# A mixture of experts streamed from memory: pairs of experts with 64 slots become quads with 32, and routing joins the experts' block

## The reference, cut to what matters

```python
N_EXPERT_GROUPS, EXPERTS_PER_GROUP, N_EXPERTS, TOP_K, D_EXPERT = 4, 8, 32, 2, 512
grp_prob = softmax(hf @ w_group_router + b_group_router);  grp_p, grp_idx = top_k(grp_prob, 1)
sel_logits = expert logits of the chosen group (8 of them)
top_p, top_i = top_k(softmax(sel_logits), 2)
gates = grp_p * top_p / sum(top_p)
# each expert over the tokens that chose it:
hid = silu(xb @ w_expert_gate[e]) * (xb @ w_expert_up[e])   # 1024 -> 512
y   = hid @ w_expert_down[e]                                # 512 -> 1024, times the gate, summed per token
x   = x + y
```

## Time and profile before

| | us |
|---|---|
| runs | 1523.35, 1523.48, 1530.56; median 1523.48 |
| span of the profiled execution | 1521.0 |
| its own end of `mix_part`, first ring load issued | 368.0 |
| routing block | 368.0 to 388.7 |
| expert block, to the next block's first work | 389.3 to 860.9 |
| TensorE busy in the whole span | 1428.1 (94%) |

### The profile page before, as it was taken

How to read it: one execution, slowest core, us unless ns; L and a number is a source line. 1 busy time by engine, 2 the same in 40 slices (tenths; PEclk the granted TensorE clock), 3 DMA queues, 4 the chain that set the end, 5 groups by cost and what they waited for, 6 DMA issues and landing times. The chain is left out here.

```text
span 1521.0 us, 23457 instructions
## 1 busy us (share of the span) xinstructions
PE 1428.1 (94%) x9837; PEld 1077.8 (71%) x9837; DVE 779.3 (51%) x1207; ACT 525.1 (35%) x726; POOL 2.9 (0%) x12
## 2 busy tenths in 40 slices
PE   6988996997799999999999799999999999999998
PEld 5988694997444444444444489789999898799997
DVE  4474765552311211211221259877777479777776
ACT  4542524332010010010000234754454455654443
POOL 0000000000000000000000000000000000000000
PEclk8999997997899999999999999999999999999999
DMA  7841000772999999999999554655664352655650
GB/s 247 267 141 38 20 4 25 221 234 118 388 421 421 421 420 421 421 421 421 421 421 420 200 175 144 167 148 172 192 193 146 119 194 84 194 168 178 193 168 28
DMA packets 192509, 349.75 MB, mean 230 GB/s; under 512 B 9164, under 2 KB 158833, under 8 KB 167570
## 3 DMA queue, kind: packets, MB, share of 16 engines
q1 hardware_dynamic: 191914, 347.59, 63.4%
q10 hardware_dynamic: 488, 0.62, 0.1%
HBM read 347.13 MB, written 3.43 MB: 230 GB/s over the span
## 5 line engine op out<-in xcount | busy, mean ns | idle before, releaser
L2616 DVE TENSOR_TENSOR w_lo<-expert_early,w_hi 128x2048 fp32r<-128x2048 f32 x72 | 164.8, 2291 | 29.3 <-ACT w_hi L2449 28.3
L1811 DVE TENSOR_TENSOR hT<-ps,hT 128x512 f32<-128x512 f32 x16 | 17.1, 1067 | 304.1 <-PE ps L1741 304.1
L1741 PE MATMUL ps<-expert_ring,w_slot 128*64 128x512 f32 x768 | 167.5, 592 | 0.0
L2449 ACT ACTIVATE w_hi<-expert_early 128x2048 fp32r<-128x2048 f32 x72 | 137.7, 1913 | 58.3 <-PE ps L2354 38.9
L1741 PEld LDWEIGHTS ps<-expert_ring,w_slot 128*64 128x64 f32 x768 | 55.6, 137 | 109.2 <-issue 109.2
L2316 PE MATMUL ps<-x_hi,w_hi 128*128 128x256 f32 x864 | 123.4, 286 | 4.6 <-DVEq L2759 4.6
L2316 PE MATMUL ps<-x_lo,w_hi 128*128 128x256 f32 x864 | 123.1, 285 | 0.3 <-DVE x_lo L2755 0.2
L2316 PE MATMUL ps<-x_hi,w_lo 128*128 128x256 f32 x864 | 121.4, 283 | 0.0
L2316 PEld LDWEIGHTS ps<-x_hi,w_hi 128*128 128x128 f32 x864 | 112.9, 192 | 8.8 <-DVEq L2759 5.0
L2316 PEld LDWEIGHTS ps<-x_lo,w_hi 128*128 128x128 f32 x864 | 112.5, 193 | 0.9 <-DVE x_lo L2755 0.8
L2316 PEld LDWEIGHTS ps<-x_hi,w_lo 128*128 128x128 f32 x864 | 111.7, 192 | 0.0
(11 more groups left out here) (487 smaller groups left out, 2263.0 us busy)
## 6 DMA issues: line engine op xcount, KB each, us to landing
expert_ring<-in_w_expert_up SPq DMA_DIRECT2D x48, 1024.0 KB, 17.6
expert_ring<-in_w_expert_down SPq DMA_DIRECT2D x48, 1024.0 KB, 20.4
expert_ring<-in_w_expert_gate SPq DMA_DIRECT2D x48, 1024.0 KB, 16.8
expert_early<-in_ffn_up SPq DMA_DIRECT2D x36, 1024.0 KB, 6.1
w_slot<-in_w_in SPq DMA_DIRECT2D x28, 1024.0 KB, 6.1
expert_early<-in_w_in SPq DMA_DIRECT2D x20, 1024.0 KB, 5.2
expert_early<-in_ffn_down SPq DMA_DIRECT2D x18, 1024.0 KB, 4.9
expert_early<-in_w_expert_gate SPq DMA_DIRECT2D x16, 1024.0 KB, 13.1
```

Source lines behind the costliest of these rows:

```text
L1741: mm = pe.matmul(m.ps[e * SLOTS:(e + 1) * SLOTS, b, :], x_pair[:, k, e * SLOTS:(e + 1) * SLOTS], w[:, e, c, :], start=(k == 0), stop=(k == ...
L1811: dve.tensor_tensor(hidden[:, :].rearrange("p (f r) -> p f r", f=FC), m.ps[:, UP, :].rearrange(apart, f=FC), silu[:, :].rearrange(apart, f ...
L2449: act.activation(w_hi[:, i % SPLIT, :], raw_slot(m, i), ACT.Copy).then_inc(S["w_hi"], 1)
L2616: dve.tensor_tensor(w_lo[:, i % SPLIT, :], raw_slot(m, i), w_hi[:, i % SPLIT, :].bitcast(F32), ALU.subtract).then_inc(S["w_lo"], 1)
```

## The change

- `SLOTS` is 32 and `OVER` 16: four experts share a bank, expert e in PSUM rows 32e to 32e+31, and the pairs become eight quads. The stationary operand of `expand` and `down` is 128x32. The extra blocks serve 32 tokens each.
- A chunk is one expert's whole matrix, 2 MiB in one transfer with 16 KB a partition. Gate, up and down of a quad wait for all four of their chunks and free them together; `half_used` is gone.
- `routing_part` and `expert_part` become `moe_part`, one block: no barrier and no clearing between them. The ranks are signalled before the counts; VectorE makes `choose(0)` at once when it has them and postpones gates, then the bookkeeping, which runs beside the first quad. The matmul of the starts comes between gate and up of quad 0. SyncE goes on from the ring's first loads to the rest with no block between.
- `over_blocks` is read at the end, behind the last quad, on each engine.
- The semaphores of `front_part` are cleared once more by GpSimd (`m.spent`).
- The pieces for the next block are loaded when `up` of the last quad is done.

```diff
-SLOTS = 64
-OVER = 8
+SLOTS = 32
+OVER = 16
...
+            if spent:
+                pool.sem_clear(range(spent[0], spent[-1] + 1))
...
+CHUNKS = tuple((name, e) for name in ("gate", "up", "down") for e in range(4))
+QUADS = N_EXP // 4
+EARLY, SLOTS_R = 2, 8
+def load_expert_chunk(sp, m, a, g):
+    i, k = divmod(g, len(CHUNKS))
+    name, e = CHUNKS[k]
+    slot = g % SLOTS_R
+    src = a[f"w_expert_{name}"][0, 4 * i + e].rearrange("(p c) n -> p c n", p=P)
+    sp.dma_start(expert_chunk(m, name, slot)[:, :, :], src).then_inc(m.landed[slot], 16)
...
+        def rows_of(e):
+            return slice(e * SLOTS, (e + 1) * SLOTS)
...
+        def expand(pe, n, b, w):
+            if n > 0:
+                pe.wait_ge(drained[b], 2 * n)
+            for j in range(2):
+                pe.wait_ge(drained[GATHER + j], n + 1)
+            for k in range(KC):
+                for e in range(4):
+                    mm = pe.matmul(m.ps[rows_of(e), b, :], x_quad[:, k, rows_of(e)], w[e][:, k, :],
+                                   start=(k == 0), stop=(k == KC - 1))
+            mm.then_inc(filled[b], 1)
...
+            for f in range(FC):
+                for j in range(2):
+                    for e in range(4):
+                        mm = pe.matmul(m.ps[rows_of(e), DOWN + j, :], hidden_T[:, f, rows_of(e)],
+                                       w[e][:, f, j * 512:(j + 1) * 512], start=(f == 0), stop=(f == FC - 1))
...
+            name, _ = CHUNKS[k]
+            if name == "gate":
                 sp.wait_ge(filled[GATE], 2 * n + 1)
             elif name == "up":
                 sp.wait_ge(filled[UP], 2 * n + 1)
             else:
                 sp.wait_ge(filled[DOWN + 1], n + 1)
...
         def over_blocks(eng):
+            eng.wait_ge(booked, 1)
             return eng.value_load(m.over_int[0:1, OVER:OVER + 1], min_val=0, max_val=OVER)
...
+                for g in range(EARLY, SLOTS_R):
+                    load_expert_chunk(sp, m, a, g)
+                for g in range(SLOTS_R, QUADS * len(CHUNKS)):
                     await_used(sp, *divmod(g - SLOTS_R, len(CHUNKS)))
                     load_expert_chunk(sp, m, a, g)
+                for s in range(EARLY):
+                    await_used(sp, QUADS - 1, len(CHUNKS) - SLOTS_R + s)
+                    for i in (2 * s, 2 * s + 1):
                         load_piece(sp, m, a, 0, i)
+                over = over_blocks(sp)
...
+                def weights(i, first):
+                    out = []
+                    for k in range(first, first + 4):
+                        g = i * len(CHUNKS) + k
+                        pe.wait_ge(m.landed[g % SLOTS_R], 16 * (g // SLOTS_R + 1))
+                        out.append(expert_chunk(m, CHUNKS[k][0], g % SLOTS_R))
+                    return out
...
+                pe.matmul(out[:, 32:64], m.c("ones"), assign[:, 0, :], start=False, stop=True).then_inc(ranks_done, 1)
+                pe.wait_ge(turn_taken, 4)
...
                 pe.wait_ge(picked, 1)
                 gather(pe, 0, pick[:, 0])
+                pe.wait_ge(rows_taken, 1)
+                for i in range(QUADS):
+                    for k, b in enumerate((GATE, UP)):
+                        expand(pe, i, b, weights(i, 4 * k))
+                        if i == 0 and k == 0:
+                            pe.wait_ge(wide_done, 1)
+                            pe.matmul(m.ps[:, B_COUNT, 0:N_EXP], blocks_wide[:, :], m.c("before")[0:N_EXP, 0:N_EXP],
+                                      start=True, stop=True).then_inc(starts_done, 1)
...
+                    down(pe, i, weights(i, 8))
+                scatter(pe, QUADS - 1)
+                over = over_blocks(pe)
...
+                dve.wait_ge(ranks_done, 1)
+                rank = m.ps[:, B_RANK, 0:64].rearrange("p (t e) -> p t e", t=TT)
+                op(dve.scalar_tensor_tensor(slot[:, :, :], rank, 1.0, assign[:, :, :], ALU.add, ALU.mult))
                 choose(0)
+                dve.wait_ge(group_out, 1)
...
+                dve_gather(dve, 0)
...
+                dve.tensor_copy(m.over_int[:, :], over_f[:, :]).then_inc(booked, 1)
...
-                routing_part(nc, m, a)
-                m.clear_banks()
-                expert_part(nc, m, a)
+                moe_part(nc, m, a)
```

More of the change, by code:

```diff
@@ L151, in clear_bank_semaphores @@
     assert ids == list(range(ids[0], ids[0] + len(ids)))
+    spent = sorted(s.num for s in m.spent)
+    assert not spent or spent == list(range(spent[0], spent[0] + len(spent)))
+    m.spent = []
     with nc.Block() as block:
@@ L1527, in _ @@
[L1527 to L1572, removed]
@@ L1673 @@
-CHUNKS = ("gate", 0), ("gate", 1), ("up", 0), ("up", 1), ("down", 0), ("down", 1)
-PAIRS = N_EXP // 2
-EARLY, SLOTS_R = 2, 8
-def expert_chunk(m, name, slot):
-    x = m.early[:, slot] if slot < EARLY else m.ring[:, slot - EARLY]
-    return x.rearrange("p e (c n) -> p e c n", c=2 if name == "down" else 4)
-def load_expert_chunk(sp, m, a, g):
-    i, k = divmod(g, len(CHUNKS))
-    name, h = CHUNKS[k]
-    slot = g % SLOTS_R
-    dst = expert_chunk(m, name, slot)
-    rows = dst.shape[2]
-    for e in range(2):
-        src = a[f"w_expert_{name}"][0, 2 * i + e].rearrange("(p c) n -> p c n", p=P)[:, rows * h:rows * (h + 1), :]
-        sp.dma_start(dst[:, e, :, :], src).then_inc(m.landed[slot], 16)
@@ new lines, in _ @@
+                mm.then_inc(turn_done, 1)
+                pe.wait_ge(m.rows_in, ROWS_IN)
+                turn_rows(pe, m, B_ROWS).then_inc(rows_done, 1)
+                pe.wait_ge(assigned, 1)
+                out = m.ps[:, B_RANK, :]
+                pe.matmul(out[:, 0:32], m.c("before"), assign[:, 0, :], start=True, stop=True)
+                pe.matmul(out[:, 32:64], m.c("before"), assign[:, 1, :], start=True, stop=False)
+                pe.matmul(out[:, 32:64], m.c("ones"), assign[:, 0, :], start=False, stop=True).then_inc(ranks_done, 1)
@@ new lines, in _ @@
+                op(dve.tensor_copy(blocks_wide[:, :], blocks_col[:, :].to_broadcast([N_EXP, P]))).then_inc(wide_done, 1)
+                dve.wait_ge(starts_done, 1)
+                start = m.ps[:, B_COUNT, 0:N_EXP]
+                op(dve.tensor_tensor(ends[:, :], start, blocks[:, :], ALU.add))
+                for t in range(TT):
+                    dve.scalar_tensor_tensor(scratch[:, t, :], start, float(SLOTS), slot[:, t, :], ALU.mult, ALU.add)
+                dve.drain()
+                op(dve.tensor_scalar(scratch[:, :, :], scratch[:, :, :], float(-SLOTS), None, ALU.add))
```

390 lines of the change are left out of this document (185 added, 205 removed).

## The result

| | before | after |
|---|---|---|
| runs, median (lowest to highest), us | 1524.89 (1520.49 to 1530.56), 7 runs | 1515.48 (1514.94 to 1518.77), 7 runs |
| ratio, 95% interval | | 0.9936 [0.9916, 0.9956] |
| span of the profiled execution, us | 1521.0 | 1513.4 |
| first ring load issued | 368.0 | 368.8 |
| last `down` starts | 846.0 | 834.8 |

A second comparison gave 1515.88 us and 0.9949 [0.9931, 0.9967]. So the change is worth 0.5 to 0.6%, 8 to 10 us; the two intervals together allow 0.3 to 0.8%. The profiled spans differ by 7.6 us, and 7.8 us are there at the next block's start.

A forecast was written before the change was run, and what follows sets the result against it. TensorE paced the kernel before, memory nearly level; after, transfers would bind. Refill 3.2 plus rate 4.4, less 0.8 for the last `down` and 0.8 for the register, gave 6.0 us: 1517.5 us, range 1509 to 1528.

The forecast's parts named there:

- The bound: Expert block: TensorE paces before at 28.8 us a pair, memory nearly level at 29.9; after, transfers bind.
- Quarters: TensorE's 32-wide matmuls: four side by side in 0.43 to 0.46 us, so a quad costs TensorE 28.8 us.
- Steady refills at nothing: Ring during the quads: each refill is issued behind 10 us of queued transfers, so the queue stays full.
- The refill gap, 3.2 us: Ring after routing: an earlier gate issues the first refill at 395 instead of 401 us, gaining 3.2 us.
- The 2.5 us counted as spare: First refill after routing: its data were to flow 2.5 us before the ring drained at 398.9 us.
- The rate, 4.4 us: Ring loads with 16 KB rows: 425 GB/s instead of 421, 463.8 us instead of 468.2, gain 4.4 us.
- The first rival: Longer rows pay fully (430 GB/s) or the clock stays up at the last `down`: down to 1509.8 us; chance 0.24.
- Landing: Last ring chunk: lands at 836.9 us instead of 844.5.
- The tail: From the last chunk's landing to the next block, start forecast at 854.9 us: costs 0.8 for `down`, 0.8 for the register.
- The cold start: Last `down`: starts at 1.2 GHz after TensorE's wait and loses 2.3 us, 0 if the clock is still up.
- a register read on VectorE: Block's end: the count's read moves behind the last scatter, 0.55 + 0.21 us, costing 0.8 us.
- From span to median: Whole kernel: 2.5 us between profiled span and median of runs, added to 1515.0 to give 1517.5 us.

The follow-up runs named there:

- pairs16k: The kernel before with its pairs kept, but each chunk one expert's whole matrix in 16 KB rows; 1525.87 us, ratio 1.0004 to the kernel before.
- expert_major: The changed kernel with gate and up's loops exchanged, so one expert's eight matmuls follow each other; 1606.27 us.
- late_refill: The changed kernel with SyncE's first refill made to wait for the end of VectorE's bookkeeping; 1519.03 us, ratio 0.9956 to the kernel before.
- rows4k: The changed kernel with each chunk loaded by four transfers with rows of 4 KB; 1537.18 us.
- after_again: The changed kernel run once more, unaltered, as base for a neighbour on the same chip; 1515.88 us, ratio 0.9949 to the kernel before.
- warm_down: The changed kernel with twelve idle matmuls on constants ahead of the last `down`; 1515.1 us, ratio 0.9938 to the kernel before.
- early_branch: The changed kernel with TensorE's count read and branch ahead of the last `down`, VectorE's read before its last additions; 1513.55 us, ratio 0.9921 to the kernel before.
- both_ends: The changed kernel with TensorE's branch ahead of the last quad's up, early reads, twelve idle matmuls before the last `down`; 1513.52 us, ratio 0.9925 to the kernel before.
- no_branch: The changed kernel without the extra blocks and without any engine's count read or branch; 1513.36 us, ratio 0.9923 to the kernel before.

## Why the prediction was right, and where not

The forecast was 1517.5 us in a range of 1509 to 1528. The result is 1515.48. The gain was forecast at 6.0 us and is 7.6 in the profiled spans and 9.4 in the medians; the forecast's base was 1523.48, three runs, and the median of seven is 1524.89. The 2 us between 1517.5 and 1515.48 are a sum of misses in both directions: the rate gave 3.3 us more, the start took 0.8, the unplaced 0.5 and the tail 0.2 of it back, and the second block and the step from span to median make the rest. The forecast had "within 0.5%" as likelier than "faster"; both comparisons put the change at or just beyond that bound, 0.51 and 0.64% faster.

- **The bound.** Right: TensorE paced the kernel before, and memory was 1.1 us a pair behind it. pairs16k shows it from the other side. One reading was off by a slice: the slices of the earlier trace rows at 420 to 421 GB/s are the 12th to the 22nd; the one ahead of them, 388, holds the gap after the routing.
- **Quarters.** Right: four loads in 0.43 us at full clock. expert_major shows what it hung on. A quad kept TensorE busy some 33 us (113.79 of 200 us, at 58.8 us a quad), not 28.8, as the groups start at the low clock; behind the transfers this costs nothing.
- **Steady refills at nothing.** Right: 428 GB/s from 440 to 820 us. For a whole group TensorE idled up to 13.7 us.
- **The refill gap, 3.2 us.** Right in size, by a path 2 us later than worked out. The gather began at 383.59 instead of 381.3 and the refill was issued at 396.88 instead of 395. 0.8 us lie ahead of the block. The logits' matmuls took 7.0 us, where they had taken 4.6: the granted clock was 0.50 from 368 to 372 us, where it had been 0.84. `assign` came at 381.64, where it had been 378.44. The 2.5 us counted as spare took it up; 424 GB/s in the window shows that little was left. late_refill shows that the gap costs what the window loses.
- **The rate, 4.4 us: the step that was mis-sized.** The prediction said "I take 425, because the two rows that speak for more are a short and a mixed one". It measured 428, and the term is 7.7 us. The estimate with a fixed cost for each row gave exactly 428, and rows4k gave its other point. The doubt about its sources had moved the number, where it should have widened the range. The 425 that the prediction quoted beside its own is 3 short as well; the measurement decides. The first rival was to decide from 426.5 GB/s. By the rate it came in, by the clock it did not, so its 1509.8 was not reached.
- **Landing.** Forecast 836.9, and TensorE started on the last chunk at 834.84: 3.3 earlier by the rate, 0.8 later by the start, 0.5 later unplaced.
- **The tail.** Forecast 9.4 + 7.8 + 0.8 = 18.0 us, measured 18.25. The cold start cost 2.85 us, not 2.3, as the low clock lasted some 5.9 us from 834.84. The 4.6 us of the prediction were counted from 390, where its window begins; from the gather's start at 390.75 its rows give 3.9, so the term came nearer to the measured loss than its own rows would have put it. Behind `down` it took 8.3 instead of 8.6. The extra over before, 0.5 where 0.8 was forecast, was booked as a register read on VectorE. The runs showed another carrier: TensorE's own read (from 848.4) comes ahead of its jump, which ends last. Before, the jump began 1.2 us ahead of VectorE's last addition (856.7, 857.89); after, 0.3 ahead (849.3, 849.59). It was 0.4 us shorter this time (3.83, 3.45), which gives the 0.5. Nearly the right amount, incomplete mechanism. The prediction cited the Trainium skill (TensorE: Matmul & The Clock Gate, HAM oscillation) for groups that restart cold after waits for transfers. The trace agrees. The second quad's gate, for one, starts at 441.68 after 10.7 us of idling with its loads 0.85 us apart, and they are 0.43 apart only from 444.91 on; the mean clock is 0.77 from 600 to 800 us.
- **From span to median.** The 2.5 us between span and median became 2.1; by the seven runs of before they were 3.9. That is the scatter of executions, and it is why the medians differ by more than the spans.

## What to carry to other kernels

When one engine paces and another resource is nearly level with it, cost both: here the quads with the old rows brought 0.2%, the new rows with the old pairs nothing, and both together 0.5 to 0.6%. Look at the bytes of a row before taking a full DMA share for the limit, and keep the share and the rate apart. Once a stage is bound by transfers, what counts is a gap in the queue and what follows the last landing: a cold clock, a register read, a jump; put these inside the wait, where they cost nothing as long as it covers them.

## What the runs showed of the hardware that was not expected

- TensorE's COMPARE_BRANCH over the extra blocks' code took 3.4 to 3.9 us (3831 ns before, 3448 in after, 3405 in after_again, 3882 in warm_down), and 6.46 and 5.93 us in early_branch and both_ends, while weights were streaming. The same branch took 0.05 to 0.07 us on the other engines, and TensorE's branch that skipped nothing took 0.08 us (early_branch, L1798). The Trainium skill (Runtime: NRT & Kernel Launch, Instruction fetch mechanics) says that a taken branch to code outside the pages already fetched waits for a transfer of that code. The traces agree. The transfers by queue within TensorE's jump, in after (849.3 to 852.8 us) and in early_branch (826.9 to 833.4; packets, MB, share):

```profile
q8 instruction: 1, 0.02, 1.8%
```

```profile
q1 hardware_dynamic: 764, 2.53, 98.4%
q8 instruction: 1, 0.02, 1.0%
```

All eleven profiles with a long jump have exactly one such packet of 16 KB in it. It starts 0.9 to 1.5 us after the jump does and takes 0.9 to 1.5 us, and the jump ends 1.4 to 1.5 us behind it. no_branch, without the jump, has none between 849 and 856.9 us. In early_branch and both_ends the packet starts only 4.0 and 3.5 us into the jump, among the weights, and the 1.4 us behind it are the same. So the longer jump is a later packet, and not the last quad's code that is skipped in addition there. Why the other engines are spared was not tried.
- At 4, 8 and 16 KB a row the steady rate was 409, 421 and 428 GB/s, with the DMA share at 1.01 to 1.03 throughout.
